# Two buffers for a pair's expert outputs, and its scatter shared by the two following experts

## The chip, the cores and the metric

The kernel runs on one core of a Trainium2 chip. The metric is the device time of one execution in microseconds (us): the median of three runs.

## The reference

One layer of a hybrid backbone over 128 context tokens and 256 latent tokens of width 2048: token mixers (attention and a gated long convolution), then a mixture of 16 SwiGLU experts. The mixers fill the first 1340 us and aren't touched. The mixture is

```python
aff = jax.nn.softmax((xs @ p['w_router']).astype(jnp.float32), axis=-1)
g, idx = lax.top_k(aff.T, cap)
xe = xs[idx]
a = jnp.einsum('ecd,edf->ecf', xe, p['w_exp_gate'])
u = jnp.einsum('ecd,edf->ecf', xe, p['w_exp_up'])
ye = jnp.einsum('ecf,efd->ecd', jax.nn.silu(a) * u, p['w_exp_down']) * g[..., None].astype(h.dtype)
out = jnp.zeros((n, D), h.dtype).at[idx.reshape(-1)].add(ye.reshape(-1, D))
```

Each expert chooses 16 context and 32 latent tokens (48 slots). Its weights are three matrices of 2048x1024 in float32, 25.2 MB in all.

## The kernel before

**Experts in order.** TensorE runs through the experts 0 to 15. For each it makes the gate and up products (`L1548`, 16 row blocks of weights in 8 pairs, 16 rows of the trace for a pair), then turns the hidden values into columns (`L1577`), then makes the down products (`L1587`, 4 pairs). Between, ScalarE applies SiLU (`L2101`), VectorE multiplies (`L3299`, `products`) and copies the turned columns (`L3303`). ScalarE copies the down products out of PSUM into `ye` (`L2112`). The stretch from an expert's last gate/up product to its first down product is called its turn here.

**Weights.** SP issues the loads in order. From expert 3 on there is a ring of four slots of 2 MB, a pair each (`L600`); a load waits until TensorE has released its slot (`piece_used`, and `gu_done` and `down_done` for the last of a kind). Experts 0 to 2 have more places, among them the first 2048 columns of `XX`; its last piece is expert 2's fourth gate/up pair. Experts 14 and 15 have a function of their own (`last_two`, `L1628` and `L1663`).

**Scatter.** Two experts 2p and 2p+1 are a pair. Their outputs stand in `ye`, 4 column blocks of 512, one expert at partitions 0 to 47, the other at 64 to 111. The matrix `s_cur` puts them back to 384 token rows (3 row tiles m) with the gate values in it. The products (`scatter`, `L1509`) go to PSUM, and VectorE adds them to `facc` (`accumulate`, `L3294`). An item is one row tile of one half of the columns, that is two products and two accumulations; there are six items t to a pair. Before, all six of pair p stand in expert 2p+2: items 0 to 3 behind the gate/up pairs 2, 4, 6 and 8, item 4 behind them and item 5 behind the turned columns, both in the turn. Product n = 2t+u goes to bank 4 + n % 3 and waits until product n-3 has been accumulated:

```python
                    pe.wait_ge(e_acc, pair * 12 + (n + 1))
                    mm(bank(4 + n % 3), s_cur[0:64 + SLOTS, m * P:(m + 1) * P],
                       ye[0:64 + SLOTS, 2 * i + u, :], start=True, stop=True).then_inc(e_sc, 1)
```

**Other work beside the experts.** In experts 3 and 5 TensorE also gathers inputs of experts 6 to 15 (`gather_rest`, `L1486` and `L1487`, banks 6 and 7), five items behind the first gate/up pairs and three in the turn. The odd experts turn the next pair's scatter matrix in their turn (`scatter_matrix`, `L1498`). Expert 13 broadcasts the rows of the last gate in four places of its gate/up loop (`broadcast_gates`, `L1325`, from diagonals that VectorE makes at `L3082`; VectorE copies the results at `L3093`). Engines take their instructions in the order written; on TensorE, ScalarE and VectorE the experts of three passes are a hardware loop (`Fori`).

## Time and profile before

| | |
|---|---|
| Median of 3 runs | 2291.67 us (2289.37 to 2293.55) |
| Profiled execution, span | 2289.1 us |
| Own time of the profiled execution | not given beside its span |
| TensorE busy | 2173.7 us (95%) |
| VectorE busy | 1078.6 us (47%) |
| ScalarE busy | 370.7 us (16%) |
| Bytes moved | 647.7 MB, mean 283 GB/s |
| Granted TensorE clock, mean | 0.991 |
| Experts' stage | about 1340 to 2289 us |

Busy time of TensorE is the time in which a product was under way. Where a stage is paced by transfers, TensorE is busy for much of the span as well, so its share alone doesn't name the bound; the rate of the transfers in a stretch does. A row of the chain names what ended a wait, in order of time.

### The profile page before, as it was taken

The numbers are of one execution on the slowest core, as the hardware profiler recorded it, in microseconds if no ns is written. First come the engines' busy times: TensorE is split into PE (matmuls) and PEld (weight loads), VectorE is DVE, ScalarE is ACT, GpSimd is POOL, SyncE is SP. The second block draws the span as 40 slices with busy tenths as digits, with TensorE's granted clock in tenths as the row PEclk, the third lists the DMA queues.
The fourth block names the chain that finished last, engine by engine and source line by source line (L and its number), as shares of the span: only waits on it lengthen the run. The fifth ranks groups of instructions, "written<-read, shape, count | busy, mean of one in ns | idle before, by whom it ended". The sixth has DMA issues, their size and how long they took to land.

```text
span 2289.1 us, 26778 instructions
## 1 busy us (share of the span) xinstructions
PE 2173.7 (95%) x10755; PEld 1373.2 (60%) x10755; DVE 1078.6 (47%) x1701; ACT 370.7 (16%) x937; POOL 137.5 (6%) x143
## 2 busy tenths in 40 slices
PE   6999999999999999999999999999998888989997
PEld 3389974467899999999986853333332222222223
DVE  6198998776777678766654331100111110102114
ACT  3011110012443441100000221010110000000002
POOL 0001100013111110000000001100000000000000
PEclk9999999999999999999999999999999999999999
DMA  9954553342442334443463569999999999999997
GB/s 393 427 223 187 209 200 143 152 191 81 191 178 114 145 148 190 179 184 148 184 248 124 195 256 396 402 413 428 421 428 420 427 429 427 424 429 427 426 422 311
DMA packets 54293, 647.71 MB, mean 283 GB/s; under 512 B 6150, under 2 KB 6696, under 8 KB 9128
## 3 DMA queue, kind: packets, MB, share of 16 engines
q1 hardware_dynamic: 51992, 637.66, 67.8%
q10 hardware_dynamic: 2192, 8.52, 0.9%
q8 instruction: 78, 1.28, 0.2%
q14 instruction: 31, 0.25, 0.0%
HBM read 642.47 MB, written 3.69 MB: 282 GB/s over the span
## 4 chain that ended last, share of the span: by engine, by line
PE 74%; DMA 19%; DVE 3%; issue 1%; DVEq 1%; ACT 1%; ACTq 0%; POOL 0%; SPq 0%; POOLq 0%
PE PS L898 28%; DMA ring<-in_w_gate_up 15%; PE PS L1548 8%; PE PS L1587 7%; PE PS L756 5%; PE PS L1376 4%; PE PS L1075 3%; PE PS L1361 2%; DMA ring<-in_w_down 2%; PE PS L1509 2%; PE PS L1062 2%; PE PS L745 1%; PE PS L1663 1%; PE PS L1628 1%; DMA ring<-in_w_ada 1%
## 5 line engine op out<-in xcount | busy, mean ns | idle before, releaser
L1548 PE MATMUL PS<-ring,RF 128*48 128x512 f32 x1568 | 357.8, 596 | 49.5 <-DMA ring<-in_w_gate_up 47.8
L2431 DVE SCALAR_TENSOR_TENSOR RG<-ring,SM,RG 128x512 f32<-128x512 f32 x450 | 329.0, 769 | 17.4 <-issue 1.3
L1548 PEld LDWEIGHTS PS<-ring,RF 128*48 128x48 f32 x1568 | 97.3, 123 | 295.9 <-issue 192.9
L898 PE MATMUL PS<-RB,ring 128*128 128x192 f32 x1376 | 233.3, 327 | 0.6 <-ACT RE L1803 0.6
L898 PEld LDWEIGHTS PS<-RB,ring 128*128 128x128 f32 x1376 | 224.9, 190 | 6.8 <-ACT RE L1803 1.9
L3294 DVE TENSOR_TENSOR RB<-RB,PS 128x512 f32<-128x512 f32 x84 | 56.6, 685 | 360.2 <-PE PS L1509 360.1
L1587 PE MATMUL PS<-ring,RF 128*48 128x512 f32 x832 | 189.5, 613 | 5.3 <-DMA ring<-in_w_down 3.0
L3299 DVE TENSOR_TENSOR RG<-RF,PS 48x512 f32<-48x512 f32 x32 | 22.1, 690 | 300.9 <-ACT RF L2101 268.3
L1587 PEld LDWEIGHTS PS<-ring,RF 128*48 128x48 f32 x832 | 56.0, 127 | 136.0 <-issue 127.7
L898 PE MATMUL PS<-RE,ring 128*128 128x192 f32 x768 | 130.1, 326 | 0.0
L756 PE MATMUL PS<-ring,RB 128*128 128x512 f32 x288 | 126.9, 593 | 0.0
L898 PEld LDWEIGHTS PS<-RE,ring 128*128 128x128 f32 x768 | 124.9, 190 | 0.1
L756 PEld LDWEIGHTS PS<-ring,RB 128*128 128x128 f32 x288 | 53.6, 190 | 62.8 <-issue 62.8
L1509 PE MATMUL PS<-RC,RF 112*128 112x512 f32 x168 | 88.2, 652 | 0.0
L2101 ACT ACTIVATE RF<-PS 48x512 f32<-48x512 f32 x28 | 16.6, 592 | 429.8 <-PE PS L1548 398.3
L898 PE MATMUL PS<-XX,RF 128*128 128x192 f32 x448 | 76.4, 326 | 0.0
L898 PEld LDWEIGHTS PS<-XX,RF 128*128 128x128 f32 x448 | 73.4, 190 | 0.0
L2112 ACT ACTIVATE RC<-PS 48x512 f32<-48x512 f32 x56 | 33.1, 592 | 231.5 <-PE PS L1587 230.8
L1628 PE MATMUL PS<-ring,RF 128*48 128x512 f32 x256 | 57.8, 597 | 5.3 <-DMA ring<-in_w_gate_up 5.3
L2275 POOL COPY RF<-RE 128x768 f32<-128x768 f32 (+1 forms) x15 | 12.4, 827 | 801.7 <-PE PS L1548 680.4
L1509 PEld LDWEIGHTS PS<-RC,RF 112*128 112x128 f32 x168 | 29.4, 194 | 49.7 <-issue 43.7
L1361 PE MATMUL PS<-ring,RC 128*128 128x512 f32 x128 | 56.0, 593 | 0.0
(468 smaller groups left out, 2889.3 us busy)
## 6 DMA issues: line engine op xcount, KB each, us to landing
ring<-in_w_gate_up SPq DMA_DIRECT2D x104, 2048.0 KB, 14.6
ring<-in_w_ada SPq DMA_DIRECT2D x48, 2048.0 KB, 8.7
ring<-in_w_down SPq DMA_DIRECT2D x44, 2048.0 KB, 15.7
ring<-in_w_in SPq DMA_DIRECT2D x38, 2048.0 KB, 7.9
ring<-in_w_gate_up SPq DMA_DIRECT2D x28, 1024.0 KB, 9.0
ring<-in_w_attn_o SPq DMA_DIRECT2D x8, 2048.0 KB, 7.5
ring<-in_w_out SPq DMA_DIRECT2D x8, 2048.0 KB, 7.7
ring<-in_w_down SPq DMA_DIRECT2D x16, 1024.0 KB, 9.8
```

Source lines behind the costliest of these rows:

```text
L756: last = mm(bank(b0 + m), lhs[:, h * HK + k, m * P:(m + 1) * P], ring[:, (n + h) % 4, k, :], start=(h == 0 and k == 0), stop=(h == 1 and k ...
L898: last = mm(bank(b, TH), w(k), x(k), start=start and k == 0, stop=k == kn - 1, skip_group_check=not start)
L1062: last = mm(bank(0), hT[:, h * HK + k, 0:P], ring[:, n % 4, k, :], start=h == 0 and k == 0, stop=h == 1 and k == HK - 1)
L1075: last = mm(bank(b, 2 * P), x(k), w(k), start=start and k == 0, stop=k == HK - 1, skip_group_check=not start)
L1361: last = mm(bank(2 + q % 2), mixT[:, h * HK + k, 0:P], ring[:, n % 4, k, :], start=h == 0 and k == 0, stop=h == 1 and k == HK - 1)
L1376: last = mm(bank(b, 2 * P), x(k), w(k), start=start and k == 0, stop=k == HK - 1, skip_group_check=not start)
L1509: mm(bank(4 + n % 3), s_cur[0:64 + SLOTS, m * P:(m + 1) * P], ye[0:64 + SLOTS, 2 * i + u, :], start=True, stop=True).then_inc(e_sc, 1)
L1548: last = mm(bank(n, p0=64 * u, p1=64 * u + SLOTS), xeT[:, 0, kk, :] if first else x_cur[:, kk, :], homes[home_of(at, 2 * i + u)][:, k * FF ...
L1587: last = mm(bank(2 + i, p0=64 * u, p1=64 * u + SLOTS), hTe[:, k, :], homes[home_of(at, 16 + k)][:, (2 * i + u) * NC_:(2 * i + u + 1) * NC_ ...
L1628: last = mm(bank(n, p0=64 * u, p1=64 * u + SLOTS), x_cur[:, kk, :], pieces[:, (q + u) % 8, k * FF + n * NC_:k * FF + (n + 1) * NC_], start ...
L2431: last = stt(out=acc[c], in0=w, scalar=cond[:, kk, c:c + 1], in1=acc[c], op0=ALU.mult, op1=ALU.add)
L3294: tt(facc[:, m, q], facc[:, m, q], bank(4 + n % 3), ALU.add).then_inc(e_acc, 1)
```

## The change

`ye` becomes two buffers that the pairs use in turn, the old one and the first 2048 columns of `XX`, which GpSimd clears during expert 2 once the last weights there have been used. Pair p's items 0 to 2 (the first half of the columns) stand in expert 2p+2, items 3 to 5 in expert 2p+3, each behind the gate/up pairs 2, 4 and 6 of its expert. The products of an item use banks 4 and 5 alone, and each waits for the accumulation of the product two before. Pair 6 keeps its six items in expert 14, with the two banks. The waits of the gather on accumulations go, since bank 6 is no longer shared. The loops over three passes become straight code on TensorE, ScalarE and VectorE.

```diff
--- before.py
+++ after.py
@@ -140,7 +140,7 @@
         mixT = view(RC, 0, KT, T)
         rT = view(RC, 0, KT, T)
         selG, sel_cur = view(RC, 0, MT, NE // 2, P), view(RC, 3072, MT, P)
-        ye = view(RC, 4096, 4, NC_)
+        ye_of = [view(RC, 4096, 4, NC_), view(XX, 0, 4, NC_)]
 
         hN = view(RE, 0, MT, D)
         dec = view(RE, 6144, MT, HYW)
@@ -1474,11 +1474,6 @@
 
                 if k == 0:
                     pe.wait_ge(sel2_ready, 3)
-                    pe.wait_ge(e_acc, 3 + 12)
-                elif k == 8:
-
-                    pe.wait_ge(e_acc, 3 + 24)
-                    pe.wait_ge(gat2_a, k - 1)
                 elif k > 1:
                     pe.wait_ge(gat2_a, k - 1)
                 b, kk, n = 6 + k % 2, paired(k), NE2 * CAPL
@@ -1505,18 +1500,18 @@
                 for u in range(2):
                     n = 2 * t + u
 
-                    pe.wait_ge(e_acc, pair * 12 + (n + 1))
-                    mm(bank(4 + n % 3), s_cur[0:64 + SLOTS, m * P:(m + 1) * P],
-                       ye[0:64 + SLOTS, 2 * i + u, :], start=True, stop=True).then_inc(e_sc, 1)
+                    pe.wait_ge(e_acc, 3 + pair * 12 + (n - 1))
+                    mm(bank(4 + u), s_cur[0:64 + SLOTS, m * P:(m + 1) * P],
+                       ye_of[pair % 2][0:64 + SLOTS, 2 * i + u, :], start=True, stop=True).then_inc(e_sc, 1)
 
             def expert(e, pair=None, turn=None, at=3, rest=None, gates=False):
 
                 first = at == 0
 
                 def beside(t):
-                    if pair is not None:
-                        scatter(pair, t // MT, t % MT, t)
-                    if gates and t < 4:
+                    if pair is not None and t < MT:
+                        scatter(pair, e % 2, t, e % 2 * MT + t)
+                    if gates:
                         broadcast_gates(2 * t, 2, ones2, diag2_ready, g2_bc, g2_used)
 
                 def landing(q):
@@ -1565,7 +1560,6 @@
 
                 if gates:
                     pe.wait_ge(g2_used, 8)
-                beside(4)
                 if turn is not None:
                     scatter_matrix(turn)
                 between(0)
@@ -1577,7 +1571,6 @@
                         last = mm(o, src, i_, start=True, stop=True) if j == 0 else trp(o, src, i_)
                     last.then_inc(e_htr, 1)
                     between(1 + n)
-                beside(5)
                 pe.wait_ge(e_hT, e * 2 + 1)
                 pe.wait_ge(e_hT, e * 2 + 2)
                 for k in range(HK):
@@ -1595,15 +1588,13 @@
             expert(0, at=0)
             expert(1, at=1, turn=0)
             expert(2, at=2, pair=0)
-            expert(3, turn=1, rest=0)
+            expert(3, pair=0, turn=1, rest=0)
             expert(4, pair=1)
-            expert(5, turn=2, rest=8)
+            expert(5, pair=1, turn=2, rest=8)
             pe.wait_ge(gat2_a, KT)
-            with pe.Fori(3, NE // 2 - 2) as p:
+            for p in range(3, NE // 2 - 1):
                 expert(p * 2, pair=p - 1)
-                expert(p * 2 + 1, turn=p)
-            expert(NE - 4, pair=NE // 2 - 3)
-            expert(NE - 3, turn=NE // 2 - 2, gates=True)
+                expert(p * 2 + 1, pair=p - 1, turn=p, gates=p == NE // 2 - 2)
 
             def last_two():
 
@@ -2089,7 +2080,7 @@
                 act.wait_ge(sg_tr, p + 1)
                 A(s_cur, bank(4, T), ACT.Copy).then_inc(sc_st, 1)
 
-            def expert(e, odd, turn=None, rest=None, first=False):
+            def expert(e, odd, turn=None, rest=None, zeroed=None):
                 if rest is not None:
                     for i in range(5):
                         gathered_rest(rest + i)
@@ -2104,24 +2095,24 @@
                 if rest is not None:
                     for i in range(5, 8):
                         gathered_rest(rest + i)
-                if first:
-                    act.wait_ge(zeros, 1)
+                if zeroed is not None:
+                    act.wait_ge(zeros, zeroed)
                 for i in range(2):
                     act.wait_ge(down_done, e * 2 + (i + 1))
                     for u in range(2):
-                        last = A(ye[64 * odd:64 * odd + SLOTS, 2 * i + u, :],
+                        last = A(ye_of[e // 2 % 2][64 * odd:64 * odd + SLOTS, 2 * i + u, :],
                                  bank(2 + i, p0=64 * u, p1=64 * u + SLOTS), ACT.Copy)
                     last.then_inc(e_yc, 1)
 
             for k in range(KT):
                 gathered(k)
-            expert(0, 0, first=True)
+            expert(0, 0, zeroed=1)
             expert(1, 1, turn=0)
-            expert(2, 0)
+            expert(2, 0, zeroed=3)
             expert(3, 1, turn=1, rest=0)
             expert(4, 0)
             expert(5, 1, turn=2, rest=8)
-            with act.Fori(3, NE // 2 - 1) as p:
+            for p in range(3, NE // 2 - 1):
                 expert(p * 2, 0)
                 expert(p * 2 + 1, 1, turn=p)
 
@@ -2277,7 +2268,7 @@
 
             next_inputs(0)
             pool.wait_ge(piece_used, 16)
-            g_.memset(ye[:, :, :], 0.0).then_inc(zeros, 1)
+            g_.memset(ye_of[0], 0.0).then_inc(zeros, 1)
             pool.wait_ge(piece_used, RELEASES + 10)
             g_.memset(selG[:, :, :, :], 0.0).then_inc(zeros, 1)
             pool.wait_ge(sg_ready, MT)
@@ -2285,6 +2276,8 @@
             next_inputs(1)
             g_.memset(facc[:, :, :], 0.0).then_inc(facc_zero, 1)
             pair_selection(1)
+            pool.wait_ge(piece_used, 2 * RELEASES + 8)
+            g_.memset(ye_of[1], 0.0).then_inc(zeros, 1)
             next_inputs(2)
             next_inputs(3)
             pair_selection(2)
@@ -3291,7 +3284,7 @@
                     n = 2 * t + u
                     q = slice((2 * i + u) * NC_, (2 * i + u + 1) * NC_)
                     dve.wait_ge(e_sc, pair * 12 + (n + 1))
-                    tt(facc[:, m, q], facc[:, m, q], bank(4 + n % 3), ALU.add).then_inc(e_acc, 1)
+                    tt(facc[:, m, q], facc[:, m, q], bank(4 + u), ALU.add).then_inc(e_acc, 1)
 
             def products(e, n):
 
@@ -3309,8 +3302,8 @@
 
             def expert(e, pair=None, with_gates=False):
                 for t in range(4):
-                    if pair is not None:
-                        accumulate(pair, t // MT, t % MT, t)
+                    if pair is not None and t < MT:
+                        accumulate(pair, e % 2, t, e % 2 * MT + t)
                     if with_gates:
                         if t == 0:
 
@@ -3320,9 +3313,6 @@
                 products(e, 1)
                 products_to_columns(e, 0)
                 products_to_columns(e, 1)
-                if pair is not None:
-                    accumulate(pair, 1, 1, 4)
-                    accumulate(pair, 1, 2, 5)
 
             dve.wait_ge(gat_ca, KT)
             V.memset(SM[:, 121:122], 0.0).then_inc(e_acc, 3)
@@ -3335,14 +3325,17 @@
             normalised_l(NE1, NE, lambda t: selL[:, t, NE1:NE, :].rearrange("p e s -> p (e s)"), sel2_ready)
             expert(1)
             dve.wait_ge(facc_zero, 1)
-            expert(2, pair=0)
-            expert(3)
-            with dve.Fori(2, NE // 2 - 2) as p:
+            for p in range(1, NE // 2 - 1):
                 expert(p * 2, pair=p - 1)
-                expert(p * 2 + 1)
-            expert(NE - 4, pair=NE // 2 - 3)
-            expert(NE - 3, with_gates=True)
-            expert(NE - 2, pair=NE // 2 - 2)
+                expert(p * 2 + 1, pair=p - 1, with_gates=p == NE // 2 - 2)
+            for t in range(4):
+                accumulate(NE // 2 - 2, t // MT, t % MT, t)
+            products(NE - 2, 0)
+            products(NE - 2, 1)
+            products_to_columns(NE - 2, 0)
+            products_to_columns(NE - 2, 1)
+            accumulate(NE // 2 - 2, 1, 1, 4)
+            accumulate(NE // 2 - 2, 1, 2, 5)
 
             products(NE - 1, 0)
             products(NE - 1, 1)
...
```

(Three places of expert 14 and 15 in which only the buffer's name changes are left out.) Line numbers of the new kernel are up to 10 smaller: scatter `L1504`, gate/up `L1543`, columns `L1571`, down `L1580`, gather `L1481` and `L1482`, accumulate `L3287`, products `L3292`, diagonals `L3075`.

TensorE, from the last 16 gate/up products (two pairs) of expert 2 into expert 3 ( `L1577` are the turned columns, `L1587` the down products, `L1486` and `L1487` a gather item). Before:

```order
L1548 MATMUL PS<-ring,RF 48x512 x16
L1509 MATMUL PS<-RC,RF 128x512 x4
L1577 MATMUL PS<-KC,RG 128x48 x8
L1509 MATMUL PS<-RC,RF 128x512 x2
L1587 MATMUL PS<-ring,RF 48x512 x32
L1548 MATMUL PS<-ring,RF 48x512 x8
L1486 MATMUL PS<-RF,RA 128x320 x2
L1487 MATMUL PS<-KC,RA 128x160
L1548 MATMUL PS<-ring,RF 48x512 x8
L1486 MATMUL PS<-RF,RA 128x320 x2
L1487 MATMUL PS<-KC,RA 128x160
```

The same stretch now:

```order
L1543 MATMUL PS<-ring,RF 48x512 x16
L1571 MATMUL PS<-KC,RG 128x48 x8
L1580 MATMUL PS<-ring,RF 48x512 x32
L1543 MATMUL PS<-ring,RF 48x512 x8
L1481 MATMUL PS<-RF,RA 128x320 x2
L1482 MATMUL PS<-KC,RA 128x160
L1543 MATMUL PS<-ring,RF 48x512 x8
L1504 MATMUL PS<-RC,RF 128x512 x2
L1481 MATMUL PS<-RF,RA 128x320 x2
L1482 MATMUL PS<-KC,RA 128x160
```

The six scatter products around the turned columns are gone from expert 2's turn, and the first two of the moved ones stand behind expert 3's second pair, ahead of a gather item.

VectorE, expert 13 (`L3082` or `L3075` make diagonals, four instructions each; `L3093` or `L3086` copy a broadcast). Before, from the accumulations at the end of expert 12's turn:

```order
L3294 TENSOR_TENSOR RB<-RB,PS 128x512 x4
L3082 TENSOR_SCALAR RF<-KC,MODS 128x128 x8
L3093 COPY RE<-PS 128x2x2x128
L3082 TENSOR_SCALAR RF<-KC,MODS 128x128 x4
L3093 COPY RE<-PS 128x2x2x128
```

The same now:

```order
L3287 TENSOR_TENSOR RB<-RB,PS 128x512 x2
L3075 TENSOR_SCALAR RF<-KC,MODS 128x128 x8
L3086 COPY RE<-PS 128x2x2x128
L3075 TENSOR_SCALAR RF<-KC,MODS 128x128 x4
L3086 COPY RE<-PS 128x2x2x128
L3075 TENSOR_SCALAR RF<-KC,MODS 128x128 x4
L3287 TENSOR_TENSOR RB<-RB,PS 128x512 x2
```

In the first list the accumulations belong to expert 12's scatter; in the second they are expert 13's own, and stand ahead of its first two diagonals and between its copies.

## Rows read from the trace of the kernel before

**Rows 1.** The page, part 2: GB/s in 40 equal slices of 57 us
```profile
GB/s 393 427 223 187 209 200 143 152 191 81 191 178 114 145 148 190 179 184 148 184 248 124 195 256 396 402 413 428 421 428 420 427 429 427 424 429 427 426 422 311
```

**Rows 2.** Windows over turns: stretch; busy PE, PEld, DVE, ACT, POOL; PEclk; DMA; GB/s
```profile
1484.00:1504.00 20.00, 19.51 (x78) 6.83 (x78) 5.76 (x10) 0.59 (x1) 0.00 (x0) 0.91 0.95 381
...
1542.00:1562.00 20.00, 20.00 (x97) 8.93 (x95) 2.10 (x4) 4.32 (x10) 1.28 (x2) 1.00 1.01 428
...
1603.00:1623.00 20.00, 19.51 (x77) 6.53 (x77) 5.30 (x10) 0.59 (x1) 0.00 (x0) 0.91 0.99 406
...
1723.00:1743.00 20.00, 19.51 (x81) 6.21 (x81) 4.47 (x8) 0.89 (x2) 0.00 (x0) 0.91 0.98 404
...
1841.00:1861.00 20.00, 19.51 (x87) 6.66 (x87) 4.62 (x9) 2.33 (x4) 0.00 (x0) 1.00 1.01 429
...
1959.00:1979.00 20.00, 19.51 (x82) 6.21 (x82) 4.12 (x8) 1.24 (x3) 0.00 (x0) 0.91 0.99 411
...
2135.00:2155.00 20.00, 17.85 (x79) 7.17 (x79) 3.26 (x6) 1.31 (x3) 0.51 (x1) 0.91 1.01 425
...
2194.00:2214.00 20.00, 19.51 (x79) 6.57 (x79) 5.55 (x10) 0.59 (x1) 0.00 (x0) 0.91 0.99 409
```

**Rows 3.** Chain that ended last, experts 6 and 8: start us, us, what
```profile
1716.59 3.64 PE PS L1548 x16
...
1834.77 3.64 PE PS L1548 x16
...
1838.41 1.93 PE PS L1509 x4
...
1846.17 13.90 PE PS L1587 x64
```

**Rows 4.** Timeline of SP's issues: start us, us, queue, line, what, count
```profile
1733.44 26.73 SPq L600 DMA_DIRECT2D ring<-in_w_gate_up  x8
...
1849.97 28.12 SPq L600 DMA_DIRECT2D ring<-in_w_gate_up  x8
```

**Rows 5.** Timeline of TensorE, expert 2's turn: start us, us, work, [idle before]
```profile
1482.56 3.70 PE L1509 MATMUL PS<-RC,RF 112*128 112x512 f32 x8
...
1491.75 8.79 PE L1587 MATMUL PS<-ring,RF 128*48 128x512 f32 x40
```

**Rows 6.** Timeline of TensorE, expert 3: first pair, last pair, first down products
```profile
1505.53 3.60 PE L1548 MATMUL PS<-ring,RF 128*48 128x512 f32 x16
...
1538.89 3.64 PE L1548 MATMUL PS<-ring,RF 128*48 128x512 f32 x16 [0.70 <-DMA ring<-in_w_gate_up]
...
1548.81 13.94 PE L1587 MATMUL PS<-ring,RF 128*48 128x512 f32 x64
```

**Rows 7.** Timeline of expert 13: four rows of TensorE, one of VectorE
```profile
2097.30 7.07 PE L1548 MATMUL PS<-ring,RF 128*48 128x512 f32 x32 [1.71 <-ACT RC L2112]
...
2110.47 3.64 PE L1548 MATMUL PS<-ring,RF 128*48 128x512 f32 x16 [0.61 <-DMA ring<-in_w_gate_up]
...
2130.05 3.64 PE L1548 MATMUL PS<-ring,RF 128*48 128x512 f32 x16 [0.67 <-DMA ring<-in_w_gate_up]
...
2139.84 5.73 PE L1587 MATMUL PS<-ring,RF 128*48 128x512 f32 x17 [0.50 <-DVE RF L3303]
...
2106.07 0.86 DVE L3082 TENSOR_SCALAR RF<-KC,MODS 128x128 f32<-128x128 f32 x4
```

**Rows 8.** Timeline of expert 14's turn: TensorE's scatters, VectorE's accumulations
```profile
2192.35 3.70 PE L1509 MATMUL PS<-RC,RF 112*128 112x512 f32 x8
...
2197.94 3.49 PE L1509 MATMUL PS<-RC,RF 112*128 112x512 f32 x4
...
2194.38 0.69 DVE L3294 TENSOR_TENSOR RB<-RB,PS 128x512 f32<-128x512 f32 x1 [0.17 <-PE PS L1509]
...
2198.33 1.27 DVE L3294 TENSOR_TENSOR RB<-RB,PS 128x512 f32<-128x512 f32 x2
```

**Rows 9.** Timeline of TensorE: expert 8's first products, after the loop's branch
```profile
1800.51 3.64 PE L1548 MATMUL PS<-ring,RF 128*48 128x512 f32 x16 [1.25 <-DMA ring<-in_w_gate_up]
```

More of the change, by code:

```diff
@@ L1654, in last_scatter @@
                             pe.wait_ge(e_acc, pair * 12 + 3 + (n - 3))
-                        mm(bank(4 + n % 4), s_cur[0:64 + SLOTS, m * P:(m + 1) * P], ye[0:64 + SLOTS, c, :],
+                        mm(bank(4 + n % 4), s_cur[0:64 + SLOTS, m * P:(m + 1) * P], ye_of[pair % 2][0:64 + SLOTS, c, :],
                            start=True, stop=True).then_inc(e_sc, 1)
@@ L2142, in outputs @@
                     for u in range(1 if c == 3 and d == 1 else 2):
-                        last = A(ye[64 * d:64 * d + SLOTS, c, u * 2 * P:(u + 1) * 2 * P],
+                        last = A(ye_of[1][64 * d:64 * d + SLOTS, c, u * 2 * P:(u + 1) * 2 * P],
                                  bank(B_DOWN[c][d], 2 * P, p0=64 * u, p1=64 * u + SLOTS), ACT.Copy)
```

2 lines of the change are left out of this document (1 added, 1 removed).

## The prediction

> **What bounds the kernel now.** I read the page's slices first [rows 1]. From the 25th slice of 57 us to the last but one, the transfers run at 396 to 429 GB/s. That is the expert stage: 16 experts of 25.2 MB each, which at 428 GB/s is 58.8 us an expert. So the question is not how busy TensorE is, but when TensorE's lateness leaves the queue empty.
>
> The windows of 20 us laid over the turns show it [rows 2]. A turn is the stretch between an expert's last gate/up product and its first down product. Over expert 8's turn the rate is 429 GB/s, which I take as the full rate. Over those of experts 2, 4, 6, 10 and 14 it is 381, 406, 404, 411 and 409. The empty time is (429 - rate)/429 x 20 us: 2.24, 1.07, 1.17, 0.84 and 0.93 us. Expert 13's window (425) gives 0.19.
>
> Why one turn costs and another does not can be seen in the chain and in SP's issues. Expert 6's last gate/up pair is taken up at 1716.59 as it lands, and the first slot of the down products is issued again at 1733.44 [rows 3, 4]. That is D = 16.85 us, and 1.17 us are lost. For expert 8 it is 1834.77 to 1849.97, D = 15.20 us, and nothing is lost. (The last pair's products take 3.6 us, so the turn itself begins 3.6 us after the first of these times.) The ring holds four pairs, so up to some D the three pairs still under way cover the gap. I put the limit at 16.85 - 1.17 = 15.7 us; it lies above 15.2 in any case. Loss = D - 15.7. The difference between the two turns is partly TensorE's clock: the granted clock is 0.91 over the window of expert 6 and 1.00 over that of expert 8 [rows 2]. A mean of 0.91 over 20 us is 3.4 us at the lower level of 1.2 GHz, hence 1.7 us of delay.
>
> **The change, part by part.** TensorE's products stay the same in number. A scatter item (two products) takes 1.93 us on TensorE, as the row at 1838.41 shows [rows 3]. There are six for a pair, 11.5 us, all in the even expert; now 5.8 us stand in each of the two experts.
>
> *Even experts 2, 4, 6, 8, 10, 12.* Three items leave, and all three stood in the turn. Expert 2's turn is 1482.56 to 1491.75, 9.2 us [rows 5]. Without the items what is left is the SiLU, the products and the turning of the columns; the nearest row is expert 8's turn (1838.41 to 1846.17, 7.8 us [rows 3]) less 3.8 us for the item at its head and the one at its end, so about 4 us. D falls to about 3.6 + 4 + 3.5 = 11 us, far below 15.7. The losses of experts 2, 4, 6 and 10 vanish: 2.24 + 1.07 + 1.17 + 0.84 = **-5.3 us**. The rest of the shorter turn is worth nothing, since the next pair has not landed; nor are the scatters' places within the gate/up loop.
>
> *Experts 3 and 5.* These also carry eight gather items each and get three scatter items on top. Before, expert 3's gate/up starts at 1505.53 and its last pair could start at 1538.89 - 0.70 = 1538.19, 32.7 us later, just before it landed [rows 6]. So there is no spare time there. The new start is at a landing, since expert 2 ends five microseconds earlier. The last pair then ends 32.7 + 3 x 1.93 + 3.6 = 42.1 us after the first one landed. Seven landings take 34.3 us (expert 13 waits for landings at 2110.47 and 2130.05, four pairs apart, 4.9 us each [rows 7]). So the last pair ends 7.8 us after its landing. The turn, with three gathers in it, stays 1548.81 - 1542.46 = 6.35 us [rows 6] (1542.46 is 1538.89 plus the 3.57 after which the next item follows a pair's products). The first down pair takes 13.94/4 = 3.5 us. D = 7.8 + 6.35 + 3.5 = 17.6, less 15.7: a loss of 1.9 us each: **+3.8 us** for the two. The bounds on the limit (15.2, and 16.2 if half of expert 6's slow clock is counted otherwise) give 1.4 to 2.4 each.
>
> *Expert 13.* It already broadcasts the gate rows in four places and now has three scatter items as well. It starts at 2097.30, having waited for ScalarE, 1.5 us after its pair landed (2110.47 - 3 x 4.9 = 2095.8) [rows 7]. On VectorE the first accumulation now stands ahead of the diagonals that TensorE's first broadcast needs; before, they were made long ahead. In expert 14 an item begins at 2192.35 and its second accumulation ends at 2194.38 + 0.69 = 2195.07, 2.7 us later [rows 8]; the first diagonal takes 0.86 more [rows 7]. TensorE would be free after 1.93, so it waits about 1.7 us, once. The gate/up loop lasts 8 x 3.45 + 3 x (1.93 + 1.93) + 1.7 = 40.9 us, and ends 1.5 + 40.9 - 34.3 = 8.1 us after the last landing. (The products of a pair follow each other at 13.94/4 = 3.45 to 3.5 us [rows 6].) The turn with the fourth broadcast stays 2139.84 - (2130.05 + 3.6) = 6.2 us [rows 7], the first down pair 3.5. D = 17.9, loss 2.2. The granted clock over this turn is 0.91 in the trace of before [rows 2]; as there, I count 1.7 us for it: 3.9, less the 0.19 lost already, **+3.7 us**. Without the slow stretch it is 2.0.
>
> *Expert 14* keeps its six items in one expert, but with two banks instead of three. After its turn's copies, the fifth item's first product could start at 2197.94, ahead of VectorE's two accumulations at 2198.33 [rows 8]; with two banks each product waits for one of them. That is 1.0 us (the accumulation's 0.64 and the wait ahead of it); its D is over the limit already (it loses 0.93), so **+1.0 us**. Below, 0.
>
> *What costs nothing.* One memset of 128x2048 on GpSimd stands ahead of expert 3's inputs, in the gate/up loop of expert 2, where GpSimd idles. The removed waits in the gather were met long before. ScalarE's copies go to another buffer, the same in number. Behind expert 14 nothing is changed; the stream's delay passes to the end one to one.
>
> The loops of TensorE, ScalarE and VectorE over three passes are written out. Between two passes TensorE waits 1.25 us, at 1800.51, for a landing [rows 9]: an instruction stall there would be hidden. The Trainium skill ("Runtime: NRT & Kernel Launch", Instruction fetch mechanics) says that a taken branch forces a fetch and stalls, and that kernels therefore do better unrolled; by it the change should gain at each removed branch. By the row it gains nothing, as whatever there is lies under the landing.
>
>
> **The sum**: -5.3 + 3.8 + 3.7 + 1.0 = +3.2 us. The profiled execution spans 2289.1 us, which would become 2292.3; the runs' median is 2291.7 (2289.4 to 2293.6), 2.6 above that span. On the median: 2294.9, and I say 2294.5, since expert 13's loss contains a stretch of slow clock that may fall elsewhere.
>
> **The rivals.** (a) *The holes close and no new ones open.* For it: the total work is equal, and each expert then needs about 29 + 6 + 4 + 14 = 53 us against 58.8. Against: experts 3 and 5 are over 58.8 by the gathers. It needs a limit of D above 17.9, where the trace shows a loss at 16.85. The price is -5.3: 2286.4. If expert 13 alone still loses, 2288 to 2290. Chance 0.1 for the first, which is the case of faster.
> (b) *Half clock in the turns of experts 3 and 5 too, or in both*, the side of slower. Place: the 6.35 us turn, where TensorE has small products with gaps; the clock is at 1.00 over expert 3's turn now, but at 0.91 over six of the other seven shown [rows 2]. As D is then over the limit, each costs 1.7 us in full: one makes the sum 4.9, two 6.6 (2298). From one on it passes 0.2%. A larger wait for VectorE in expert 13 would act alike. Chance 0.22.
> (c) *The change does nothing measurable because the dips are the memory's own.* For it: there is no dip at expert 8's turn, though its code is that of expert 6. Against: its clock explains that, and the losses follow D. 2291.7, chance 0.1, within the case of same.
> (d) *The written-out loops gain something.* For it: two branches back on each of three engines go. Against: TensorE's next products wait for a landing there [rows 9]. If each of the two waits of 1.25 us hid nothing but the branch, the sum would be +0.7: 2292.4. The Trainium skill's rule on branches (same page and section) would act in this way. Chance 0.04, within same.
> My forecast, a sum between -1 and +4.6, has 0.54.
>
> **How the numbers follow.** A measurement can tell about 0.2% (4.6 us) from no change. Faster 0.10 is (a). Slower 0.22 is (b). The rest, 0.68, is the forecast, (c) and (d). The likeliest case's own range, from the bounds (1.4 to 2.4 twice, 2.0 to 4.2, 0 to 1.1) is 2291 to 2296.5. The range for 8 in 10 takes in most of (c) and part of both others: 2288 to 2298.5.
>
> **What would show it.** In the new profile, windows of 20 us over the turns of experts 2, 4, 6 and 10 should be at 425 or more, and those of 3 and 5 at about 390. Expert 13's turn should be at 345 to 385, and its first broadcast should wait for VectorE's diagonals. Expert 14's should be at about 390. The even turns should last about 4 us. The prediction is wrong if the windows of 3 and 5 stay at 428 (then the limit of D is wrong, or the start of expert 3 is earlier than I think), or if the clock is at half level in them.

## The result and the profile after

The changed kernel takes 2298.45 us in the median of ten runs (2295.45 to 2300.51), the kernel before 2292.18 (2289.37 to 2294.33). The ratio is 1.0029, 95% interval 1.0021 to 1.0037: 6.6 us slower, with 4.8 to 8.5 in the interval (the medians are 6.3 apart). The profiled execution spans 2296.5 us, 7.4 more than the one of before. Of these, 2.4 lie in front of any instruction that the change moves: expert 1's first product starts at 1406.54, and at 1404.18 before.

The slices, the line that answers to [rows 1], with the page's first line and its line on the instruction fetches (78 packets, 1.28 MB before):

```profile
span 2296.5 us, 26593 instructions
...
GB/s 388 426 217 195 202 202 147 151 190 81 188 180 111 147 147 190 177 184 147 184 255 116 202 261 395 405 428 413 428 417 428 428 427 428 428 428 427 389 413 317
...
q8 instruction: 85, 1.39, 0.2%
```

Where the dips were spread over the even experts, there are now two early ones (413 and 417) and two late ones (389 and 413; 427 and 426 before). The windows of 20 us over the turns of experts 2, 3, 4, 5, 6, 8, 10, 12, 13 and 14, with the columns of [rows 2]:

```profile
1486.00:1506.00 20.00, 15.81 (x76) 5.94 (x77) 1.41 (x3) 2.52 (x5) 0.00 (x0) 1.00 1.02 427
1548.00:1568.00 20.00, 20.00 (x96) 8.46 (x96) 1.41 (x3) 5.09 (x11) 0.28 (x1) 1.00 0.94 383
1604.00:1624.00 20.00, 18.45 (x74) 6.34 (x74) 1.48 (x4) 1.69 (x3) 0.48 (x1) 0.83 1.01 429
1667.00:1687.00 20.00, 20.00 (x95) 8.50 (x95) 1.41 (x3) 5.10 (x11) 1.28 (x2) 1.00 0.97 395
1724.00:1744.00 20.00, 18.06 (x75) 5.97 (x75) 1.41 (x3) 1.84 (x4) 0.07 (x1) 0.83 1.00 424
1841.00:1861.00 20.00, 17.39 (x74) 6.40 (x74) 1.48 (x4) 2.21 (x4) 0.59 (x1) 0.91 1.01 429
1960.00:1980.00 20.00, 15.89 (x74) 5.61 (x74) 1.53 (x4) 2.17 (x4) 0.64 (x1) 1.00 1.01 430
2078.00:2098.00 20.00, 17.03 (x73) 5.95 (x72) 1.41 (x3) 2.37 (x5) 0.00 (x0) 0.91 1.01 428
2141.00:2161.00 20.00, 17.86 (x72) 6.53 (x72) 3.48 (x6) 0.96 (x2) 0.62 (x2) 0.83 0.78 318
2200.00:2220.00 20.00, 18.66 (x70) 6.39 (x70) 6.04 (x10) 0.59 (x1) 0.55 (x1) 0.91 0.95 388
```

The even turns are at 424 to 430 even where the clock is 0.83. The loss, (429 - rate)/429 x 20 us, is 2.1 us at expert 3, 1.6 at expert 5, 5.2 at expert 13 and 1.9 at expert 14, where it was 0, 0.05, 0.2 and 0.9.

An even turn now, expert 4's, and expert 3's end (timeline of TensorE, as in [rows 5, 6]):

```profile
1505.33 3.64 PE L1543 MATMUL PS<-ring,RF 128*48 128x512 f32 x16 [3.06 <-DMA ring<-in_w_gate_up]
...
1539.86 7.07 PE L1543 MATMUL PS<-ring,RF 128*48 128x512 f32 x32
1546.86 0.55 PE L1493 MATMUL PS<-KC,RC 128*128 128x128 f32 x3
...
1553.21 7.07 PE L1580 MATMUL PS<-ring,RF 128*48 128x512 f32 x32
...
1599.93 3.64 PE L1543 MATMUL PS<-ring,RF 128*48 128x512 f32 x16 [0.65 <-DMA ring<-in_w_gate_up]
1604.13 0.77 PE L1571 MATMUL PS<-KC,RG 48*128 48x48 f32 x5 [0.56 <-DVE RG L3292]
...
1606.84 6.14 PE L1580 MATMUL PS<-ring,RF 128*48 128x512 f32 x14 [0.50 <-DVE RF L3296]
```

SP's issue into the slot that expert 3's first down pair gives back:

```profile
1557.08 3.83 SPq L600 DMA_DIRECT2D ring<-in_w_gate_up  x2
```

Expert 4's last pair ends at about 1603.5 and its down products begin at 1606.84, a turn of 3.4 us (about 4 forecast). Expert 3's first pair waits 3.06 us for its landing, so that expert is paced by transfers at its start, as forecast. Its eighth pair ends at 1546.86 and its down products begin at 1553.21, a turn of 6.35. With seven landings in 34.3 us, D = 1557.08 - (1505.33 + 34.3) = 17.5; 1.8 of it lie beyond the limit of 15.7, and the window lost 2.1.

Expert 13 (TensorE, VectorE's accumulations and diagonals in its first place, and SP's issue into the first down slot):

```profile
2102.82 3.64 PE L1543 MATMUL PS<-ring,RF 128*48 128x512 f32 x16 [0.64 <-DMA ring<-in_w_gate_up]
2106.40 1.98 PE L1504 MATMUL PS<-XX,RF 112*128 112x512 f32 x4
2109.95 1.98 PE L1325 MATMUL PS<-RF,RE 128*128 128x512 f32 x4 [1.56 <-DVE RF L3075]
...
2118.86 1.98 PE L1504 MATMUL PS<-XX,RF 112*128 112x512 f32 x4
2120.68 1.88 PE L1325 MATMUL PS<-RF,RE 128*128 128x512 f32 x4
...
2140.14 1.98 PE L1325 MATMUL PS<-RF,RE 128*128 128x512 f32 x4
...
2146.49 4.51 PE L1580 MATMUL PS<-ring,RF 128*48 128x512 f32 x10 [0.49 <-DVE RF L3296]
...
2108.42 0.69 DVE L3287 TENSOR_TENSOR RB<-RB,PS 128x512 f32<-128x512 f32 x1 [0.17 <-PE PS L1504]
2109.02 1.65 DVE L3075 TENSOR_SCALAR RF<-KC,MODS 128x128 f32<-128x128 f32 x8
...
2152.92 0.34 SPq L661 DMA_DIRECT2D ring<-in_w_gate_up  x1
```

The first broadcast waits 1.56 us for VectorE's diagonals (1.7 forecast), the second not. D is 2152.92 - (2102.82 + 6 x 4.9) = 20.7 us, and 20.7 - 15.7 = 5.0 is close to the 5.2 that the window lost. The first down pair takes 2152.92 - 2146.49 = 6.4 us instead of 3.5. Those 2.9 us go with the half clock, which was on for longer here than in the trace of before (0.83 against 0.91 in the window).

Expert 14's turn (TensorE, from its first scatter product to its first down product):

```profile
2199.58 3.89 PE L1504 MATMUL PS<-RC,RF 112*128 112x512 f32 x8
...
2206.28 3.41 PE L1504 MATMUL PS<-RC,RF 112*128 112x512 f32 x4 [1.04 <-DVE RB L3287]
2209.63 5.57 PE L1619 MATMUL PS<-ring,RF 128*48 128x512 f32 x24
```

The sixth item waits 1.04 us for VectorE's accumulations, and the stretch lasts 2209.63 - 2199.58 = 10.05 us. Before, it lasted 2201.36 - 2192.35 = 9.01 without such a wait, at the same clock (0.91 in both windows):

```profile
2201.36 8.93 PE L1628 MATMUL PS<-ring,RF 128*48 128x512 f32 x40
```

### The profile page after: what moved, and what is told of

It reads as the page before. It is cut to its first block, busy times and chain, and to the rows that moved or that the text cites. A ratio compares the mean times of both kernels' runs of the same rounds, so it can differ in the third digit from the quotient of the medians.

```text
span 2296.5 us, 26593 instructions
## 1 busy us (share of the span) xinstructions
PE 2175.7 (95%) x10755; PEld 1376.9 (60%) x10755; DVE 1079.5 (47%) x1701; ACT 370.7 (16%) x937; POOL 140.4 (6%) x144
## 4 chain that ended last, share of the span: by engine, by line
PE 73%; DMA 19%; DVE 3%; issue 1%; DVEq 1%; ACT 1%; ACTq 0%; POOL 0%; SPq 0%; POOLq 0%
PE PS L898 28%; DMA ring<-in_w_gate_up 14%; PE PS L1543 10%; PE PS L1580 6%; PE PS L756 5%; PE PS L1376 4%; DMA ring<-in_w_down 3%; PE PS L1075 3%; PE PS L1361 2%; DMA ring<-in_w_ada 2%; PE PS L1619 2%; PE PS L1062 2%; PE PS L1504 1%; PE PS L1654 1%; PE PS L745 1%
## 5 line engine op out<-in xcount | busy, mean ns | idle before, releaser
L1543 PE MATMUL PS<-ring,RF 128*48 128x512 f32 x1568 | 357.7, 596 | 38.8 <-DMA ring<-in_w_gate_up 36.9
L3287 DVE TENSOR_TENSOR RB<-RB,PS 128x512 f32<-128x512 f32 x84 | 57.7, 687 | 575.4 <-PE PS L1504 575.3
L1543 PEld LDWEIGHTS PS<-ring,RF 128*48 128x48 f32 x1568 | 97.9, 123 | 283.7 <-issue 210.9
L1580 PE MATMUL PS<-ring,RF 128*48 128x512 f32 x832 | 197.1, 630 | 12.5 <-DMA ring<-in_w_down 7.5
L1580 PEld LDWEIGHTS PS<-ring,RF 128*48 128x48 f32 x832 | 61.0, 129 | 139.1 <-issue 115.1
L3292 DVE TENSOR_TENSOR RG<-RF,PS 48x512 f32<-48x512 f32 x32 | 22.1, 690 | 124.2 <-ACT RF L2092 92.8
L1619 PE MATMUL PS<-ring,RF 128*48 128x512 f32 x256 | 57.2, 597 | 4.2 <-DMA ring<-in_w_gate_up 4.2
L1794 ACT ACTIVATE RE<-PS 128x192 f32<-128x192 f32 x98 | 32.1, 328 | 134.8 <-PE PS L898 134.6
L898 PE MATMUL PS<-RC,ring 128*128 128x192 f32 x320 | 53.6, 326 | 0.0
L898 PEld LDWEIGHTS PS<-RC,ring 128*128 128x128 f32 x320 | 52.3, 190 | 0.0
```

The costliest lines, as they stand in the source:

```text
L898: last = mm(bank(b, TH), w(k), x(k), start=start and k == 0, stop=k == kn - 1, skip_group_check=not start)
L1543: last = mm(bank(n, p0=64 * u, p1=64 * u + SLOTS), xeT[:, 0, kk, :] if first else x_cur[:, kk, :], homes[home_of(at, 2 * i + u)][:, k * FF ...
L1580: last = mm(bank(2 + i, p0=64 * u, p1=64 * u + SLOTS), hTe[:, k, :], homes[home_of(at, 16 + k)][:, (2 * i + u) * NC_:(2 * i + u + 1) * NC_ ...
L1619: last = mm(bank(n, p0=64 * u, p1=64 * u + SLOTS), x_cur[:, kk, :], pieces[:, (q + u) % 8, k * FF + n * NC_:k * FF + (n + 1) * NC_], start ...
L1794: A(to[j], bank(b[j % 2], TH), ACT.Copy).then_inc(unit_read, 1)
L3287: tt(facc[:, m, q], facc[:, m, q], bank(4 + u), ALU.add).then_inc(e_acc, 1)
```

## The experiments

Theory 1 is the one of the prediction: a turn costs what it takes D beyond the limit, so it matters where the items stand and how long they take, and nothing else. Theory 2: the time comes from the written-out loops, the second buffer or the start. "Stage" below is the time from expert 1's first product to the end of the profiled execution. The ratios are timed medians against the kernel before; a profile is one execution. The last ten columns are GB/s in windows of 20 us that begin within about 1 us after the end of an expert's last gate/up product, so for some turns they stand up to 2 us from those of [rows 2]. "before_look" and "after_look" are further profiles of the two kernels.

| kernel | ratio (95%) | stage us | 2 | 3 | 4 | 5 | 6 | 8 | 10 | 12 | 13 | 14 |
|---|---|---|---|---|---|---|---|---|---|---|---|---|
| before, 1st profile | | 884.9 | 381 | 429 | 406 | 428 | 401 | 425 | 412 | 430 | 425 | 415 |
| before_look1 | | 885.1 | 412 | 428 | 397 | 428 | 424 | 410 | 428 | 417 | 419 | 403 |
| before_look2 | | 883.6 | 415 | 429 | 424 | 430 | 419 | 392 | 426 | 404 | 414 | 410 |
| before_look3 | | 883.8 | 414 | 428 | 424 | 427 | 415 | 397 | 428 | 411 | 410 | 403 |
| changed, 1st profile | 1.0029 (1.0021 to 1.0037) | 889.9 | 427 | 383 | 429 | 395 | 424 | 429 | 430 | 428 | 318 | 388 |
| after_look | | 887.9 | 427 | 383 | 429 | 391 | 427 | 425 | 428 | 426 | 346 | 416 |
| after_look2 | | 889.8 | 430 | 386 | 426 | 392 | 424 | 428 | 428 | 428 | 351 | 361 |
| after_look3 | | 887.6 | 427 | 392 | 428 | 392 | 427 | 428 | 429 | 426 | 347 | 419 |
| unrolled | 1.0006 (0.9997 to 1.0015) | 882.8 | 409 | 428 | 427 | 427 | 426 | 393 | 431 | 427 | 416 | 410 |
| filler_e3_e5 | 1.0017 (1.0008 to 1.0026) | 886.0 | 408 | 370 | 425 | 385 | 416 | 413 | 429 | 428 | 418 | 410 |
| e13_free | 1.0017 (1.0008 to 1.0026) | 890.3 | 428 | 393 | 428 | 393 | 426 | 424 | 428 | 371 | 414 | 354 |
| e3_e5_free | 1.0042 (1.0029 to 1.0056) | 889.8 | 358 | 428 | 390 | 428 | 424 | 429 | 429 | 428 | 383 | 418 |
| split_2to4 | 1.0014 (1.0005 to 1.0023) | 892.2 | 361 | 427 | 350 | 430 | 428 | 428 | 428 | 406 | 419 | 351 |
| diag_first | 1.0023 (1.0014 to 1.0032) | 887.6 | 429 | 390 | 424 | 397 | 428 | 428 | 428 | 426 | 372 | 387 |
| banks14 | 1.0029 (1.0018 to 1.0039) | 887.6 | 426 | 390 | 427 | 395 | 428 | 429 | 429 | 428 | 342 | 413 |
| six_inside | 1.0010 (1.0001 to 1.0019) | 884.6 | 354 | 431 | 417 | 428 | 399 | 428 | 428 | 424 | 425 | 428 |
| six_early | 0.9993 (0.9984 to 1.0002) | 881.5 | 410 | 428 | 426 | 428 | 430 | 415 | 428 | 426 | 424 | 429 |
| mixed | 0.9996 (0.9987 to 1.0005) | 882.1 | 393 | 429 | 424 | 427 | 428 | 427 | 429 | 417 | 407 | 424 |

The ten windows account for the stage. Take from each row's stage the sum of its ten losses: what is left is 877.2 to 880.0 us in seventeen of the eighteen rows (881.6 in e3_e5_free), while the losses run from 2.1 us (six_early) to 12.2 (split_2to4). So the stages of these kernels differ by what is lost at the turns, to within about 1.5 us.

**Written-out loops alone** (`Fori` to `for` in three places of the kernel before).

> The kernel before, with the loops over three passes written out on TensorE, ScalarE and VectorE and nothing else changed. Theory 1: no change, within 1 us of the kernel before. Theory 2: 2 to 6 us slower. By the rule on taken branches in the Trainium skill (Runtime: NRT & Kernel Launch, Instruction fetch mechanics) it should be faster, if anything.

The ratio is 1.0006 and its interval holds 1. The loops are not the main cause, and the branches that go show no gain. The interval reaches 1.0015, so up to 3.4 us of cost isn't excluded by time; the stage, 882.8 us, is shorter than any of the four of before.

**The moved items' time alone, without their work.**

```diff
+                    if rest is not None and i in (1, 3, 5):
+                        for _ in range(2):
+                            mm(bank(5), ident, res[:, 0, 0:NC_], start=True, stop=True)
                     if rest is not None and i < 5:
```

> The kernel before, with two products of 128x512 that nobody reads behind the gate/up pairs 2, 4 and 6 of experts 3 and 5: the time that the moved items take there, with no scatter, no wait and no VectorE work. Theory 1: it costs what the moved items cost, 1.5 to 2.2 us each at the turns of experts 3 and 5, so +3 to +4.5 us against the kernel before, with windows of about 390 GB/s over these two turns. A rival (the moved items cost by their waits for VectorE or ScalarE, not by their time): under 1 us.

The turns of experts 3 and 5 fall to 370 and 385, losses of 2.8 and 2.1 us, though nobody waits for these products. That is no less than with the moved items themselves (2.1 and 1.6). The ratio of 1.0017 is 3.9 us, within the 3 to 4.5 expected. So TensorE's time in experts that have none to spare suffices for the cost there, and the items' waits aren't needed to explain it.

**Expert 13 without items**, and **experts 3 and 5 without items**. A list of the pairs that are shared replaces the rule:

```diff
+SPLIT = (0, 1, 2, 3, 4)          # and (2, 3, 4, 5), and (2, 3, 4)
+def items(e, pair):
+    if pair is None:
+        return {}
+    if pair in SPLIT:
+        return {t: e % 2 * MT + t for t in range(MT)}
+    return {} if e % 2 else {t: t for t in range(6)}
```

> The changed kernel, but pair 5's six items all stand in expert 12 (items 0 to 3 behind its gate/up pairs, 4 and 5 in its turn, as before the change), so expert 13 has none beside its broadcasts. Theory 1 (lateness: what a turn costs is what it takes the down slot's release beyond 15.7 us after the last gate/up landing): the loss of 5.3 us at expert 13's turn in the changed kernel's trace falls to under 0.5, expert 12's turn costs 0 to 1, so 4 to 5 us below the changed kernel, 1 to 2.5 above the kernel before. Theory 2 (the time comes from the written-out loops or from the second buffer, not from where the items stand): within 1 us of the changed kernel, 6 us above the one before.

> The changed kernel, but the six items of pair 0 stand in expert 2 and those of pair 1 in expert 4, as before the change, so experts 3 and 5 have only their gather items. Theory 1: the losses at the turns of experts 3 and 5 (2.1 and 1.6 us in the changed kernel's trace) vanish, and those of experts 2 and 4 come back (2.2 and 1.1, some tenths more as two banks make an item in the turn wait longer); the sum is within 1 us of the changed kernel. The windows of 20 us tell it: expert 3's and 5's turns at 425 or more, expert 2's at about 380, expert 4's at about 400. Theory 2: within 1 us of the changed kernel too, but with the windows of 3 and 5 as low as in the changed kernel.

With expert 13 free its loss falls from 5.2 to 0.7 us, but the six items back in expert 12 cost 2.7 there. An item in that turn waits for VectorE, as in expert 14, and the half clock fell in it:

```profile
2086.66 3.17 PE L1516 MATMUL PS<-XX,RF 112*128 112x512 f32 x4 [1.04 <-DVE RB L3302]
```

The ratio is 1.0017, 3.9 us above the kernel before, where 1 to 2.5 were expected, and 2.7 below the changed kernel, where 4 to 5 were expected. By time it lies between the two theories; the windows tell them apart. The profile, with a stage of 890.3, is of the longest of its eleven executions (2300.74 us; the median is 2294.97).

Freeing experts 3 and 5 removes their dips as expected, but the ratio is 1.0042 (five executions), 3 us above the changed kernel where 1 at most was expected. Experts 2 and 4 now lose 3.3 and 1.8 us, 5.1 together in place of the 3.7 of experts 3 and 5, so 1.4 of the 3 us stand at the turns; the rest was not located, and the intervals of the two kernels overlap.

So two banks cost about 1 us in a turn that keeps items, and this shows where the clock is the same. With the window at 0.91, expert 14 loses 0.7 to 1.2 us with three banks (before in four profiles, unrolled, filler_e3_e5, banks14) and 1.9 and 2.0 with two (changed, diag_first). At 0.91 expert 2 loses 2.2 with three banks and 3.3 and 3.2 with two. At 1.00 it loses 0.7 to 1.0 with three and 1.7 with two (mixed).

> The changed kernel with only the pairs 2, 3 and 4 shared by two experts (6 and 7, 8 and 9, 10 and 11); pairs 0, 1 and 5 stand in experts 2, 4 and 12 as before. Theory 1: all of experts 3, 5 and 13's losses go, those of 2 and 4 come back: within 1.5 us of the kernel before, the losses of experts 6 and 10 (2.0 us) being paid for by the two banks in 2, 4, 12 and 14. Theory 2: still 5 to 6 us slower than before.

The ratio is 1.0014, 3.2 us. The expectation of 1.5 us at most was missed. In the profile expert 4 lost 3.7 us with the clock at 0.83 and expert 14 another 3.6, but the profile is of the longest of the eleven executions (2298.63 us; the median is 2294.90). What agrees with the run above is that each of the four six-item turns with two banks loses, expert 12's 1.1 us at a clock of 1.00, where it lost nothing in the first profile of before.

**Diagonals first** (the wait at expert 13's first broadcast).

```diff
+                if with_gates:
+                    dve.wait_ge(wr_zero, 2)
+                    diagonals(1, 0, diag2_ready)
+                    diagonals(1, 1, diag2_ready)
                 for t in range(4):
                     if pair is not None and t < MT:
...
```

> The changed kernel, with VectorE making the first two diagonals of the last gate ahead of expert 13's first accumulation. Theory 1: TensorE's wait of 1.6 us at expert 13's first broadcast goes, D of its turn falls by as much, and so does the time: 1.6 us below the changed kernel. If the wait is covered elsewhere: no change.

The rows of its expert 13 (timeline of TensorE):

```profile
2104.51 1.98 PE L1504 MATMUL PS<-XX,RF 112*128 112x512 f32 x4
2106.33 1.88 PE L1325 MATMUL PS<-RF,RE 128*128 128x512 f32 x4
```

The wait of 1.56 us is gone, and the turn is at 372 where the four profiles of the changed kernel have 318 to 351: 2.7 us lost against 3.6 to 5.2. The time is 1.0023 against 1.0029, in the expected direction, but the intervals overlap.

**Three banks in expert 14.**

```diff
-                    pe.wait_ge(e_acc, 3 + pair * 12 + (n - 1))
-                    mm(bank(4 + u), s_cur[...
+                    three = pair == NE // 2 - 2
+                    pe.wait_ge(e_acc, 3 + pair * 12 + (n - 2 if three else n - 1))
+                    mm(bank(4 + n % 3 if three else 4 + u), s_cur[...
```

> The changed kernel, with three banks instead of two for the items that stand in expert 14. Theory 1: the turn of expert 14 is 1.0 us shorter and its loss falls from about 1.8 to 0.9, so 1 us below the changed kernel, too little for a verdict by time; the window over its turn should rise from about 390 to 409 GB/s.

The wait of 1.04 us is gone from the turn:

```profile
2195.77 3.70 PE L1505 MATMUL PS<-RC,RF 112*128 112x512 f32 x8
...
2201.36 3.35 PE L1505 MATMUL PS<-RC,RF 112*128 112x512 f32 x4
2204.64 7.79 PE L1620 MATMUL PS<-ring,RF 128*48 128x512 f32 x34
```

The stretch lasts 8.9 us against 10.05, and the window is at 413, a loss of 0.7 against 1.9 at the same clock of 0.91. So the forecast 1.0 us is there in the turn. In time it doesn't show: the ratio is 1.0029 as for the changed kernel, whose own windows there are at 388, 416, 361 and 419, with clocks of 0.91, 1.00, 0.83 and 1.00.

**All six items out of the turn**, in the kernel before.

```diff
+                    if pair is not None and 1 <= i <= 6:
+                        scatter(pair, (i - 1) // MT, (i - 1) % MT, i - 1)
...
-                beside(4)
...
-                beside(5)
```

> The kernel before (one buffer, three banks, loops kept), with all six items behind the gate/up pairs 2 to 7 of the even expert and none in its turn, in expert 14 too. Theory 1: TensorE ends its gate/up about 1.5 us later against the landings but has a turn of 4 us, so D is about 12.5, under 15.7 everywhere: the losses of experts 2, 4, 6, 10 and 14 (6.2 us) go and no new ones open: 5 to 6.5 us faster than before. Theory 2 or a rival in which each item costs by its number: no change.

This missed: 1.0010 instead of a gain of 5 us. In expert 2 the loss is 3.5 us (354). TensorE is late there through the whole loop, so a shorter turn after a longer loop gives nothing. In experts 4 and 6 the windows are at 417 and 399, with clocks of 0.91 and 0.83. Expert 8, at 0.91, and expert 10, at 1.00, lose nothing. The second pair of expert 6 and that of expert 8, which wait for their landings, and SP's issues into the slots of their first down pairs:

```profile
1688.45 3.64 PE L1546 MATMUL PS<-ring,RF 128*48 128x512 f32 x16 [1.25 <-DMA ring<-in_w_gate_up]
...
1735.06 7.17 SPq L600 DMA_DIRECT2D ring<-in_w_gate_up  x3
...
1807.19 3.64 PE L1546 MATMUL PS<-ring,RF 128*48 128x512 f32 x16 [1.25 <-DMA ring<-in_w_gate_up]
...
1852.42 7.17 SPq L600 DMA_DIRECT2D ring<-in_w_gate_up  x3
```

With six landings of 4.9 us from the second pair to the last, D is 17.2 in expert 6, a loss of 1.4, and 15.8 in expert 8, a loss of 0.05, where I had forecast 12.5. I had put the loop's added lateness too low, so D was at the limit and the half clock took it over.

**Six items behind pairs 1 to 6**, expert 2 as before, in the kernel before.

> The kernel before, with all six items behind the gate/up pairs 1 to 6 of the even experts 4 to 14 and none in the turn; expert 2, where TensorE is late anyway, keeps its items as before. Theory 1 with the size found so far: the two last pairs win back 1.45 us each, so D at full clock falls from about 15.2 to about 13.5 and stays under the limit even with the half clock (+1.7). Expert 2 keeps its 1 to 2.3 us of loss; every other even turn and expert 14's should show none. The mean loss there was 3 to 4 us in the kernel before, so 2 to 4 us faster (ratio 0.9983 to 0.9991). Rival (items inside the loop cost as much as in the turn, as in the run with six behind pairs 2 to 7): no change or slower.

Six windows of this kernel, over the turns of experts 2, 4, 6, 8, 10 and 14:

```profile
1484.00:1504.00 20.00, 19.51 (x83) 6.80 (x83) 5.95 (x10) 0.76 (x2) 0.00 (x0) 1.00 1.00 410
...
1604.00:1624.00 20.00, 17.48 (x83) 6.35 (x84) 1.40 (x3) 2.42 (x5) 0.00 (x0) 1.00 1.00 426
...
1721.00:1741.00 20.00, 17.46 (x76) 5.72 (x77) 1.41 (x3) 2.80 (x5) 0.28 (x1) 0.91 1.01 430
1840.00:1860.00 20.00, 18.72 (x84) 6.47 (x86) 1.41 (x3) 2.83 (x5) 0.29 (x1) 0.91 1.00 415
1958.00:1978.00 20.00, 18.68 (x82) 5.87 (x83) 1.34 (x3) 2.37 (x4) 0.00 (x0) 0.91 1.01 428
...
2193.00:2213.00 20.00, 19.36 (x87) 6.48 (x89) 1.41 (x3) 1.03 (x2) 0.26 (x1) 0.91 1.01 429
```

The losses outside expert 2 are nearly gone at either clock (expert 8 loses 0.7 and expert 13, which wasn't touched, 0.2), and the stage of this one profile is 881.5 us, 2.1 us under the shortest of the four of before. The timed ratio is 0.9993 (0.9984 to 1.0002): 1.6 us less, whose interval still holds 1. So the dips are shown to go, and a gain in time isn't.

> The changed kernel's two buffers, used where they can help: pairs 2, 3 and 4 shared by the experts 6 to 11; the pairs that follow with gather items or broadcasts (1, 5 and 6) wholly behind the gate/up pairs 1 to 6 of experts 4, 12 and 14; pair 0 in expert 2 as before the change. Theory 1: D under the limit at every turn but that of expert 2 (18.7, a loss of 1.5 to 3.3 us with two banks); against the mean of the looks at the kernel before, 3 us less in the turns of 4 to 12 and 0.7 less in that of 14, 0.7 more in 2: about 3 us faster, ratio 0.9983 to 0.9993. If the shared pairs cost in themselves (a second buffer, written-out loops), it is slower than the run with six items behind pairs 1 to 6.

The ratio is 0.9996 (0.9987 to 1.0005), short of the forecast 0.9983 to 0.9993 and not to be told from the run above. No cost of two buffers and written-out loops shows where they are used with room; they also bring nothing that the earlier places don't.

**Further profiles of both kernels**, for the clock and the start. The texts stand in the order before_look1, before_look2, before_look3, after_look, after_look2, after_look3.

> The kernel before again, for its profile. If the half clock falls in other turns from one execution to the next, the losses at the turns of experts 2, 4, 6, 8, 10 and 12 differ from those of the first profile: at full clock under 0.2 us (1.0 in expert 2), at half clock 1 to 1.7. If they are the kernel's own, the same turns lose the same.

> As the look before: a third profile of the kernel before, to see in how many of its even turns the clock falls and what they lose in all (5.3 us in the first profile; the mean should be nearer to 3).

> The kernel before once more, for its profile: 883 to 886 us from the first gate/up product of expert 1 to the end, and losses of 3 to 5 us in all at the turns of the even experts 2 to 12.

> The changed kernel again, for its profile. Theory 1: experts 3 and 5 lose 1.5 to 2.2 us each again, at full clock; expert 13 loses 2.3 us at full clock, 4 at half clock once, 5 at half clock twice; expert 14 about 1.8.

> The changed kernel once more, for its profile. Theory 1: from the first gate/up product of expert 1 to the end 888 to 890 us, as in the two looks so far (the kernel before: 883.6 to 885.1); what the total has beyond that lies in front of it. If the changed stage costs the 6 to 7 us of the ratio: 891 or more.

> As the look before: the losses of expert 3 and 5 between 1.5 and 2.2 again, and expert 13's between 2.3 and 5.5 by the clock.

Three windows of before_look2, over the turns of experts 4, 8 and 10:

```profile
1601.00:1621.00 20.00, 19.51 (x83) 6.90 (x83) 5.95 (x10) 0.59 (x1) 0.10 (x1) 1.00 1.00 424
...
1837.00:1857.00 20.00, 19.51 (x76) 6.51 (x76) 5.95 (x10) 0.59 (x1) 0.43 (x1) 0.91 0.96 392
1955.00:1975.00 20.00, 19.51 (x84) 6.78 (x84) 5.94 (x10) 0.86 (x2) 0.00 (x0) 1.00 1.00 426
```

Expert 8, which lost nothing in the first profile at a clock of 1.00 [rows 2], loses 1.7 us here at 0.91; experts 4 and 10, which lost 1.1 and 0.8 at 0.91, lose 0.1 to 0.2 at 1.00. The half clock moves between turns from one execution to the next, and these losses with it. At the turns of experts 2, 4, 6, 8, 10 and 12 the four profiles of before lose 5.6, 4.0, 4.4 and 4.0 us in all, 4.5 on the mean, those of the changed kernel 0.3 to 0.6. The mean of before was expected nearer to 3. Experts 3, 5 and 13 lose in the changed kernel what was expected (1.6 to 2.1 us, and 3.6 to 5.2).

The stage lasts 884.9, 885.1, 883.6 and 883.8 us before and 889.9, 887.9, 889.8 and 887.6 changed: means 884.4 and 888.8, 4.4 us apart. Expert 1's first product starts at 1404.2, 1406.4, 1404.4 and 1406.4 before, at 1406.5, 1404.2, 1404.7 and 1408.5 changed: the start scatters by 4 us with the same code in both. The mean spans, 2289.7 and 2294.8, differ by 5.1, inside the interval of the ratio (4.8 to 8.5) but at its lower end. The three later executions of the changed kernel took 2293.92, 2296.28 and 2297.91 us, all under the median of its first ten (2298.45); those of before took 2293.27, 2289.82 and 2292.13.

The starts hold one thing more. SP issues its first gate/up load at 1165.9 to 1168.1 us in the seven profiles of kernels with loops (mean 1166.9) and at 1167.5 to 1169.1 in the eleven of kernels with written-out ones (mean 1168.3), though the code of the mixers in front is the same. By expert 1's first product the means are 1405.2 and 1405.6. What makes this lag isn't shown.

## Why the prediction was wrong

I forecast no change that can be told (+3.2 us as the sum, 2294.5 us), and the kernel is 0.29% slower. The median of 2298.45 us lies above the forecast's own range (2291 to 2296.5) and just inside that for 8 in 10 (to 2298.5). The mechanism held in the stage, and the sign of each term. One term was mis-sized, and part of the timed difference lies in none of the terms. By the means of four profiles each:

- **Even turns, forecast -5.3 us**: -4.0 (4.5 lost before, 0.4 now). This is the step that failed, "The losses of experts 2, 4, 6 and 10 vanish". They do vanish, but I took the losses of one execution for the kernel's own. That execution had the half clock in four of six even turns, the three others had it in three, two and three. At full clock an even turn other than expert 2's loses 0 to 0.5, and expert 2's 0.7 to 0.8; at half clock they lose 0.6 to 1.7, and expert 2's lost 2.2.
- **Experts 3 and 5, forecast +1.9 each**: +2.0 and +1.7, and D of 17.5 against 17.6. Right. The filler products show that TensorE's time alone suffices for it.
- **Expert 13, forecast +3.7**: +3.6, between 3.6 and 5.2 lost over the four profiles against 0.6 before. Right, with its parts: the window at 346 to 351 in three profiles (318 in the first, under the 345 to 385 forecast), the wait of 1.56 us (1.7 forecast) and a turn of 6.35 (6.2). In the first profile the first down pair took 2.9 us longer at half clock, where I had 1.7.
- **Expert 14, forecast +1.0**: +0.5 on the mean, from 0.5 to 3.2 lost in single profiles. At the same clock of 0.91 it is the forecast 1.0: the wait of 1.04 us stands in all four profiles of the changed kernel, the turn of the first is 10.05 us against 9.01, and the loss is 1.9 against 0.7 to 1.2. The mean is smaller because the clock was at 1.00 there in two of the four, and at 0.91 in all four of before.
- **Unrolling and memset, forecast 0**: 1.0006 with 1 in its interval. Right within that, which still leaves room for up to 3.4 us; the run "mixed", which has the memset too, shows no cost (0.9996). The Trainium skill's rule on taken branches ("Runtime: NRT & Kernel Launch", Instruction fetch mechanics) speaks of a branch whose target has not been fetched yet. No gain from its absence shows here, and no run tells whether the loops' branches were of that kind.

The terms sum to -4.0 + 3.7 + 3.6 + 0.5 = +3.8 us, and the stage is 4.4 longer. The forecast sum with -4.0 in place of -5.3 is +4.5. So the failed step explains 1.3 us, and corrected it would still have given a time just under the 4.6 that can be told. The timed 6.6 is 2 us more than the stage. Of these 0.7 stand in front of the stage on the mean of the profiles; the other 1.5 were not located, and their cause stays open. The interval reaches down to 4.8, the start scatters by 4 us, and the profiles are few. Expert 13's term rests on one stretch of half clock in its turn; three of the four profiles had one and the first had two, so that it held in size owes something to luck.

One reading of the prediction was off without effect: for the bare turn it took two items out of expert 8's turn, in which three stood. The turn without items lasts 3.4 us against the forecast 4, as new waits for VectorE open in it.

Of the rivals, (a) fell with the windows of experts 3 and 5. (b), the side of slower, came true in sign, but not by its mechanism: the clock was at 1.00 in those turns in all four profiles. (c) fell with the repeated profiles, in which the dips follow the clock and the items. (d), at a price of -2.5 us, fell with the unrolled kernel, whose interval begins at 0.9997.

## What to carry to other kernels

Where a ring of weights paces a stage, work beside it is free up to a lateness, and costs about one to one beyond it: here D of 15.2 and 15.8 us lost nothing to speak of, 16.85 lost 1.2, 17.2 lost 1.4, 17.5 lost 2.1 and 20.7 lost 5.2. To even out the engine's load per expert is the wrong aim. What matters is how late after the last landing each expert gives its slot back, and items moved into an expert that already carries other work (the gathers, the broadcasts) land past the limit. Read that spare time expert by expert before moving work; placing the items early in the same expert's loop removed most of the same dips without a second buffer (losses of 2.1 us in the ten windows against 5.8 to 6.4), though a gain in time isn't shown. And take a loss of a microsecond from several profiles, since a clock stretch can stand where it isn't the code's.
